# Moving the f32r buffers of a one-core transformer layer to other SBUF addresses

## The reference

```python
x = x + 0.5 * swiglu(rms_norm(x, ffn1_norm), ffn1_w1, ffn1_w3, ffn1_w2)
h = rms_norm(x, mix_norm)
c_q, c_kv, k_pe, q_s, k_s, v_s = split(h @ w_in)      # 384, 256, 32, 1024, 128, 128 columns
y_mla = mla_attention(c_q, c_kv, k_pe, ...) @ w_o_mla  # 8 heads, chunk-causal mask
y_swa = swa_attention(q_s, k_s, v_s, ...) @ w_o_swa    # 16 query heads, band of 2 chunks of 64
g_mla, g_swa = split(sigmoid(h @ w_gate))
x = x + (g_mla * y_mla + g_swa * y_swa) @ w_out
x = x + 0.5 * swiglu(rms_norm(x, ffn2_norm), ffn2_w1, ffn2_w3, ffn2_w2)
return rms_norm(x, final_norm)
```

## The kernel before

| tensor | before | mod 64 | mod 2048 | after | mod 64 | mod 2048 |
|---|---|---|---|---|---|---|
| xg_hi | 32896 | 0 | 128 | 18432 | 0 | 0 |
| xg_lo | 49280 | 0 | 128 | 34816 | 0 | 0 |
| w_hi | 82048 | 0 | 128 | 51200 | 0 | 0 |
| w_lo | 90240 | 0 | 128 | 59392 | 0 | 0 |
| staged | 65664 | 0 | 128 | 83968 | 0 | 0 |
| x | 16512 | 0 | 128 | 67584 | 0 | 0 |
| h_hi | 118880 | 32 | 96 | 118848 | 0 | 64 |
| h_lo | 135264 | 32 | 96 | 135232 | 0 | 64 |
| lat_hi | 129120 | 32 | 96 | 129280 | 0 | 256 |
| lat_lo | 139360 | 32 | 96 | 139520 | 0 | 256 |
| summed | 118880 | 32 | 96 | 118784 | 0 | 0 |
| om | 151648 | 32 | 96 | 151552 | 0 | 0 |
| ks | 208992 | 32 | 96 | 223744 | 0 | 512 |
| idn | 111008 | 32 | 416 | 16992 | 32 | 608 |

## Time and profile before

### The profile page before, as it was taken

How to read it: one execution, slowest core, us unless ns; L and a number is a source line. 1 busy time by engine, 2 the same in 40 slices (tenths; PEclk the granted TensorE clock), 3 DMA queues, 4 the chain that set the end, 5 groups by cost and what they waited for, 6 DMA issues and landing times.

```text
span 1165.1 us, 14717 instructions
## 1 busy us (share of the span) xinstructions
PE 1136.4 (98%) x5110; PEld 910.2 (78%) x5110; DVE 585.3 (50%) x870; ACT 401.1 (34%) x693; POOL 182.1 (16%) x134
## 2 busy tenths in 40 slices
PE   6999999999999999998999999999999999999995
PEld 4888888888888887766777788888888888888873
DVE  6644345433446436788555564545453344334444
ACT  5322123222325225684444433332231232212242
POOL 4111011100113103322000002231110011101133
PEclk9999999999999999999999999999999999999997
DMA  6235332332224321111222122222332322322221
GB/s 216 96 103 100 108 109 90 91 105 93 91 73 129 104 91 47 55 55 39 71 73 73 59 104 91 91 101 86 102 90 91 107 92 90 102 96 91 79 65 72
DMA packets 32301, 105.43 MB, mean 90 GB/s; under 512 B 3888, under 2 KB 5328, under 8 KB 32256
## 3 DMA queue, kind: packets, MB, share of 16 engines
q1 hardware_dynamic: 31824, 104.02, 27.4%
q0 software_dynamic: 192, 0.78, 0.7%
q10 hardware_dynamic: 240, 0.05, 0.0%
HBM read 101.96 MB, written 2.88 MB: 90 GB/s over the span
## 4 chain that ended last, share of the span: by engine, by line
PE 92%; DVE 4%; ACT 2%; issue 1%; POOL 1%; DMA 0%; DVEq 0%; SPq 0%; POOLq 0%; ACTq 0%
PE bank L1097 29%; PE bank L1098 29%; PE bank L1099 29%; PE bank L1216 1%; PE bank L1248 1%; PE bank L1273 1%; DVE xg_lo L743 1%; PE bank L1206 1%; ACT probs L603 1%; PE bank L1158 0%; PE bank L1258 0%; DVE rot L986 0%; DMA x<-in_x_t 0%; DVE x L1090 0%; DVE w_lo L736 0%
## 5 line engine op out<-in xcount | busy, mean ns | idle before, releaser
L1097 PE MATMUL bank<-xg_hi,w_hi 128*128 128x512 f32 (+1 forms) x1024 | 406.5, 397 | 9.3 <-DVE xg_lo L743 7.8
L504 ACT ACTIVATE w_hi<-staged 128x1024 fp32r<-128x1024 f32 x192 | 203.5, 1060 | 589.5 <-PE bank L1099 589.5
L1099 PE MATMUL bank<-xg_hi,w_lo 128*128 128x512 f32 (+1 forms) x1024 | 399.9, 390 | 0.0
L1098 PE MATMUL bank<-xg_lo,w_hi 128*128 128x512 f32 (+1 forms) x1024 | 399.5, 390 | 0.0
L736 DVE TENSOR_TENSOR w_lo<-staged,w_hi 128x1024 fp32r<-128x1024 f32 x192 | 236.5, 1232 | 101.5 <-ACT w_hi L504 101.2
L1097 PEld LDWEIGHTS bank<-xg_hi,w_hi 128*128 128x128 f32 (+1 forms) x1024 | 192.1, 188 | 58.7 <-issue 13.4
L1099 PEld LDWEIGHTS bank<-xg_hi,w_lo 128*128 128x128 f32 (+1 forms) x1024 | 192.2, 188 | 41.5
L1098 PEld LDWEIGHTS bank<-xg_lo,w_hi 128*128 128x128 f32 (+1 forms) x1024 | 192.4, 188 | 39.1 <-issue 0.7
L391 POOL TENSOR_TENSOR h_lo<-hid,h_hi 128x512 f32 x44 | 71.2, 1618 | 571.3 <-ACT h_hi L527 542.5
L1097 PE MATMUL bank<-h_hi,w_hi 128*128 128x512 f32 x352 | 139.4, 396 | 0.1
L1098 PE MATMUL bank<-h_lo,w_hi 128*128 128x512 f32 x352 | 139.2, 396 | 0.0
(11 more groups left out here) (131 smaller groups left out, 898.0 us busy)
## 6 DMA issues: line engine op xcount, KB each, us to landing
staged<-in_ffn_w SPq DMA_DIRECT2D x119, 512.0 KB, 3.3
staged<-in_w_gate SPq DMA_DIRECT2D x16, 512.0 KB, 3.2
staged<-in_w_in SPq DMA_DIRECT2D x15, 512.0 KB, 3.3
staged<-in_ffn_w SPq DMA_DIRECT2D x16, 384.0 KB, 3.1
staged<-in_w_ob SPq DMA_DIRECT2D x8, 512.0 KB, 3.2
staged<-in_w_out SPq DMA_DIRECT2D x8, 512.0 KB, 3.4
x<-in_x_t SPq DMA_DIRECT2D x8, 256.0 KB, 5.4
staged<-in_w_oa SPq DMA_DIRECT2D x4, 512.0 KB, 3.4
```

The lines of the kernel that those rows point to most:

```text
L504: nc.scalar.activation(w_hi[:, u % SPLIT, :], staged[:, u % STAGED, :], ACT.Copy).then_inc(hi_done, 1)
L1097: nc.tensor.matmul(o, wh, hi, start=start, stop=False)
L1098: nc.tensor.matmul(o, wh, lo, start=False, stop=False)
L1099: return nc.tensor.matmul(o, wl, hi, start=False, stop=stop)
```

## The change

The small tiles (`var` to `minus_half`, `gain`, `sink` and the like, `idn`, `one`) are declared first, then the large f32r tiles with `align_bytes=2048` (`LINE`), then the rest. `h_hi` and `h_lo` get `align_bytes=64` behind an unused tile `lead` of 64 bytes; `lat_hi` and `lat_lo` get 256 behind an unused `lat_lead` of 256 bytes; `summed` and `om` get 2048. `mask_sb` and `ks` move to the end. No instruction is added, removed or moved on any engine: each engine's program is the same row by row, and only addresses differ. The last byte used is 228352 in place of 227936.

```diff
@@ -40,6 +40,7 @@
 UNIT = 8 * P
+LINE = 4 * S
 STAGED, SPLIT = 4, 2
@@ -129,37 +130,38 @@
-        def sb(name, shape, dt=f32, scope=ctx):
-            return scope.enter_context(nc.sbuf_tensor(name, shape, dt))
+        def sb(name, shape, dt=f32, scope=ctx, align=32):
+            return scope.enter_context(nc.sbuf_tensor(name, shape, dt, align_bytes=align))
...
+        var, rstd, corr, minus_half = (sb(n, [P, TT]) for n in ("var", "rstd", "corr", "minus_half"))
+        gain = sb("gain", [P, 4 * KD + 5, 1])
+        sink = sb("sink", [P, 2, 4])
+        smax, nmax, den, rden, sinkd = (sb(n, [P, 2, 4]) for n in ("smax", "nmax", "den", "rden", "sinkd"))
+
+        idn = sb("idn", [P, P])
+        one = sb("one", [P, P])
+
+        xg_hi = sb("xg_hi", [P, KD, S], f32r, align=LINE)
+        xg_lo = sb("xg_lo", [P, KD, S], f32r, align=LINE)
+        w_hi = sb("w_hi", [P, SPLIT, UNIT], f32r, align=LINE)
+        w_lo = sb("w_lo", [P, SPLIT, UNIT], f32r, align=LINE)
         x = sb("x", [P, KD, S])
-        xg_hi = sb("xg_hi", [P, KD, S], f32r)
-        xg_lo = sb("xg_lo", [P, KD, S], f32r)
         staged = sb("staged", [P, STAGED, UNIT])
-        w_hi = sb("w_hi", [P, SPLIT, UNIT], f32r)
-        w_lo = sb("w_lo", [P, SPLIT, UNIT], f32r)
...
         with ExitStack() as ffn:
-            h_hi = sb("h_hi", [P, max(PARTS), S], f32r, ffn)
-            h_lo = sb("h_lo", [P, max(PARTS), S], f32r, ffn)
+            sb("lead", [P, 16], f32, ffn)
+            h_hi = sb("h_hi", [P, max(PARTS), S], f32r, ffn, align=64)
+            h_lo = sb("h_lo", [P, max(PARTS), S], f32r, ffn, align=64)
...
             lat = sb("lat", [P, 5, S], f32, r)
-            lat_hi = sb("lat_hi", [P, 5, S], f32r, r)
-            lat_lo = sb("lat_lo", [P, 5, S], f32r, r)
+            sb("lat_lead", [P, 64], f32, r)
+            lat_hi = sb("lat_hi", [P, 5, S], f32r, r, align=256)
+            lat_lo = sb("lat_lo", [P, 5, S], f32r, r, align=256)
         with ExitStack() as r:
-            summed = sb("summed", [P, KD, 2, S], f32r, r)
+            summed = sb("summed", [P, KD, 2, S], f32r, r, align=LINE)
         gates = sb("gates", [P, KD, 2, S], f32, mix)
         with ExitStack() as r:
-            om = sb("om", [P, 2, MH // 2, S], f32r, r)
+            om = sb("om", [P, 2, MH // 2, S], f32r, r, align=LINE)
...
-        ks = sb("ks", [P, SKV, CHUNK + S], f32, mix)
...
+        mask_sb = sb("mask_sb", [P, P])
+        ks = sb("ks", [P, SKV, CHUNK + S], f32, mix)
```

More of the change, by code:

```diff
@@ L148, in trunk_layer @@
         diag = sb("diag", [P, TT, P])
[L149 to L152, removed]
         rope_sb = sb("rope_sb", [P, S])
-        mask_sb = sb("mask_sb", [P, P])
         bias = sb("bias", [P, SG // 2, SKV, BAND])
-        sink = sb("sink", [P, 2, 4])
-        smax, nmax, den, rden, sinkd = (sb(n, [P, 2, 4]) for n in ("smax", "nmax", "den", "rden", "sinkd"))
         with ExitStack() as ffn:
-            h_hi = sb("h_hi", [P, max(PARTS), S], f32r, ffn)
-            h_lo = sb("h_lo", [P, max(PARTS), S], f32r, ffn)
+            sb("lead", [P, 16], f32, ffn)
+            h_hi = sb("h_hi", [P, max(PARTS), S], f32r, ffn, align=64)
+            h_lo = sb("h_lo", [P, max(PARTS), S], f32r, ffn, align=64)
             a_rms = sb("a_rms", [P, 2, S], f32, ffn)
```

## The result

The changed kernel takes 1159.8 us (median of 4 runs, 1158.6 to 1159.88) against 1167.41 us before in the same comparison: ratio 0.9936, interval 0.9923 to 0.9949. Its profiled execution spans 1158.0 us, 7.1 us less than before. Two more comparisons are in the experiments: 1161.04 against 1166.38 us (0.9946, 0.9933 to 0.996) for the same kernel on another occasion, and 1158.41 us for a version whose h stands elsewhere.

What follows compares the result with a forecast made beforehand. TensorE, busy 98% of the 1165.1 us span, was taken to bound the kernel. Gains 7.13 + 1.30 + 0.65 + 0.3 = 9.4 us took the median from 1167.4 to 1158.0 us, range 1155.5 to 1165.6 us.

Steps and rivals of the forecast that it cites:

- main case: The whole kernel: the predicted gain of 9.4 us holds, giving 1156 to 1160.5 us; chance 71%.
- 226.6 against 233.4 ns by start-to-start distances: Dense TensorE stretches: matmuls moving xg start every 226.6 ns, those moving h, summed and om about 6.75 ns later.
- an edge every 64 bytes: Moving rows of f32r matmuls: a start off a multiple of 64 bytes touches one more piece, costing 6.67 ns.
- h, 7.13 us: Moving h to a multiple of 64 saves 6.75 ns on each of 1056 matmuls, 7.13 us.
- The 128-byte rival: If the edge is 128 bytes, h gains nothing and only 2.3 us remain, 1165.1 us; chance 10%.
- 34 and 35 pieces: Per f32r matmul: pieces of 6.67 ns each, 34 making 226.67 ns when aligned and 35 making 233.33 when not.
- summed 1.30, om 0.65, lat 0.3 us, `uv` zero: Gains from aligning the other moving operands: 192 summed, 96 om and 96 lat matmuls; the 24 of `uv` gain nothing.
- xg and w to multiples of 2048: zero: Moving xg and w from 128 to 0 modulo 2048 changes nothing; bounds 20.7 us gained or lost.
- a further gain: Rows on a multiple of 2048 are better still: xg loses another 6.75 ns, some 1135 us; chance 7%.
- colliding row starts: Rows starting at 0 modulo 2048 meet other accesses: xg costs a piece more, 11.3 us slower, 1178.7 us; chance 4%.
- The clock stretch, 1.7 us either way: Half-clock stretch in the attention stage: shorter fillers may move, drop or add one, 1.7 us; left in place.
- 16-byte lines: SBUF lines of 16 bytes: h's old address was already well placed, so the change does nothing; time stays 1167.4 us.

Runs made afterwards that it cites:

- Experiment 3: The kernel before with h_hi and h_lo alone moved by 32 bytes, to 128 modulo 2048 like xg and w: 1160.39 us against 1167.52.
- Experiments 5 and 6: Kernel before with two unused 32-byte tiles, all f32r buffers at 160 modulo 256: 1158.29 us; changed kernel with h at 0, weights at 64 modulo 256: 1183.37 us.
- the sweep: Matmul-only program, no layer, many start-address pairs of moving row and weights: 226.7 ns per matmul at distance 0, 233.3 at 32, 228.9 at 64.
- experiment 2: The changed kernel without the lead tile, h_hi and h_lo at 0 modulo 2048 instead of 64: 1158.56 us, ratio to before 0.9928.
- experiment 9: The changed kernel again, in the same rounds as its version with h at 0: 1161.04 and 1158.41 us, against 1166.38 before.
- streams (0,0) and (0,32): Matmul-only program, moving row at offset 0, weights at offset 0 or 32: 226.7 and 233.3 ns per matmul.
- experiment 8: Matmul-only program with addresses alternating between matmuls by 32 to 128 bytes: 228.3 to 234.0 ns moving row with its own weights, 230.0 to 232.8 ns crossed.

## Why the prediction came out right, and where it was wrong

The time, 1159.8 us, lies in the range and in the main case's own range (1156 to 1160.5), 1.8 us above the forecast. Point by point:

- *TensorE bounds the kernel, and a nanosecond per matmul reaches the end.* Right. Experiment 3 moves one pair of buffers by 32 bytes; its 1056 matmuls start 6.8 us earlier in sum, and the time falls by 7.1 us. In the changed kernel the busy times of VectorE and ScalarE hardly moved (585.3 to 585.6, 401.1 to 400.9 us).
- *226.6 against 233.4 ns by start-to-start distances.* Right, and reproduced by streams of matmuls alone.
- *The mechanism, an edge every 64 bytes.* Wrong. Experiments 5 and 6 take it apart from both sides: no buffer aligned and all fast, all buffers aligned and all slow. The arithmetic of 34 and 35 pieces fitted to 0.1 ns and still named the wrong cause. The step that failed is the one on xg and w: "if the phase between the two mattered, the distance would vary with the tile. It is even". The weight slices are 512 bytes apart and the rows 2048, both multiples of 256, so the phase was the same for every tile and the evenness could not speak against it. The table of addresses had the answer beside it: xg and w both at 128, all the slow tiles at 96.
- *h, 7.13 us.* The mis-sized term. The lead puts h at distance 64 to the weights, where a matmul takes 228.9 to 229.1 ns and not 226.7: 1056 x (233.4 - 228.9) = 4.75 us by the sweep, 4.5 us by the traces. In phase it was 6.8 us (experiments 2 and 3). The 128-byte rival (h gains nothing) was wrong as well; offset 128 is among the bad ones.
- *summed 1.30, om 0.65, lat 0.3 us, `uv` zero.* Measured 0.95, 0.65, 0.3 and 0.0. At four places of its stage summed has a gap of 260 to 288 ns, and behind each some ten uneven steps (224 to 237 ns) before 226.7 comes back.
- *xg and w to multiples of 2048: zero.* Right: 226.6 ns before and after. The reason given, that 64 decides, was wrong; their phase to each other is kept. That also settles the rivals of a further gain and of colliding row starts.
- *The clock stretch, 1.7 us either way.* It was in the profile before and not in the one after, 1.5 us in favour. That was luck. In the comparison of experiment 9 the changed kernel's profile has it again, and its median is 1161.04 us, outside the main case's own range. Without the stretch the terms above sum to 4.5 + 0.95 + 0.65 + 0.3 = 6.4 us, where 9.4 were predicted.

The Trainium skill's 16-byte lines ("SBUF — State Buffer", "Specifications (TRN2)"), which stood as a rival, do not describe this either: distances of 32 and 96 bytes, whole lines both, cost 6.7 ns and 0 costs none. Whether they play a part at 4 and 20 bytes, no run here separates. The Trainium skill, page "TensorE: Matmul & The Clock Gate", section "Step-by-step: what each phase is for", says that the moving operand and the weights come through two independent read ports, so that loading the next weights takes no bandwidth from the running matmul. In these runs the two are not indifferent to each other: matmuls of the same rows at the same addresses start every 226.7 or 233.3 ns by the address of the weights alone (streams (0,0) and (0,32)).

What stays open is how the two reads meet. That the distance of the addresses matters is shown; that they collide in a part of SBUF is an argument, and experiment 8 failed to say which weights a row meets.

## What to carry to other kernels

In a dense stream of f32r matmuls of 128 by 128 by 512 at full clock, put the moving rows and the weight slices at the same address modulo 256 bytes; alignment of each to 64, or to 2048, is neither needed nor enough. It is 3% of each such matmul and costs no instruction, but the good distance should be measured for another shape. When all slow buffers share one property, list what else they share, the distance to their partner above all, before a number that fits is taken for the cause.

## What the runs showed of the hardware that was not expected

- The start-to-start time of f32r matmuls depends on the addresses of both operands, between 226.7 and 240.0 ns for 512 columns at full clock.
- It is at least 13.3 ns above 512 / 2.4 = 213.3 ns even in phase. With 384 columns it is 173.3 ns, again 13.3 above 160, whether in phase or at distance 32; with 480 and 448 columns in phase it is 16.7 and 16.1 ns above.
- At half clock no dependence on the address was seen (427 ns at distance 224 in the earlier trace rows and at distance 0 in experiment 9), nor for plain float32 at distances 0, 32, 64 and 128 (429 ns).
- After small matmuls of the attention, f32r matmuls in phase mostly need four to seven steps to reach 226.7 ns (236, 228, 232, 231, then 227 in experiment 2's filler at 665.3 us), and some fillers never do.
